# A two-block transformer kernel on one Trainium2 core: the second block's mixer as a table of steps, one convolution tap on ScalarE, one routing moved ahead

## What is computed

```python
def causal_depthwise_conv(x, w, bias):      # 4 taps, 1280 channels
    y = lax.conv_general_dilated(x, w[:, None, :].astype(x.dtype), window_strides=(1,),
                                 padding=[(CONV_WIDTH - 1, 0)],
                                 dimension_numbers=('NWC', 'WIO', 'NWC'),
                                 feature_group_count=c)
    return y + bias.astype(x.dtype)
...
    xbc = jax.nn.silu(causal_depthwise_conv(xbc, conv_w, conv_b))
...
    y = ssd_scan(xh, dt, a, bm, cm) + xh.astype(jnp.float32) * d[..., None]
    y = y.reshape(b, s, SEQ_WIDTH) * jax.nn.silu(z.astype(jnp.float32))
    return rms_norm(y, out_norm).astype(z.dtype)
...
def peer_ffn(h, w_q, sub_keys, u, v):
    q = (h @ w_q).reshape(b, s, PEER_HEADS, 2, PEER_QDIM // 2)
    scores = jnp.einsum('bshic,ikc->bshik', q, sub_keys).astype(jnp.float32)
    top_s, top_i = lax.top_k(scores, PEER_TOPK)
    cand_s = top_s[..., 0, :, None] + top_s[..., 1, None, :]
    ...
    best_s, pos = lax.top_k(cand_s, PEER_TOPK)
    expert = jnp.take_along_axis(cand_i, pos, axis=-1)
    gate = jax.nn.softmax(best_s, axis=-1).astype(h.dtype)
    ...
        act = jax.nn.gelu(jnp.einsum('td,thkd->thk', xt, u[et]), approximate=False)
        return jnp.einsum('thk,thkd->td', act * gt, v[et])
```

## Time and profile before

| | |
|---|---|
| median of 3 runs | 3017.92 us (3014.9 to 3019.11) |
| the profiled execution | 3016.67 us, its span 3014.1 us |
| busy share of the span | PE 82%, DVE 47%, ACT 30%, POOL 23% |
| DMA | 1105.16 MB, 367 GB/s over the span |
| ACT table loads | 119, 152.7 us |

### The profile page before, as it was taken

One profiled execution on the slowest core, in us unless ns is written; L12 is line 12 of the kernel. 1 busy time (PEld: TensorE's weight loads), 2 busy tenths in 40 slices (PEclk: granted clock), 3 DMA queues, 4 the chain that ended last, 5 costly groups with the idle time before them and its releaser, 6 DMA issues.

```text
span 3014.1 us, 33539 instructions
## 1 busy us (share of the span) xinstructions
PE 2473.4 (82%) x11846; PEld 1329.6 (44%) x11846; DVE 1425.9 (47%) x3374; ACT 889.7 (30%) x2348; POOL 699.4 (23%) x626
## 2 busy tenths in 40 slices
PE   9999765657999965666798998898987989877777
PEld 8776311113978421212574445454543545422222
DVE  3363100002355201000348876678657786677674
ACT  0231100000122100000235554457334583344333
POOL 4020000001211000000003553324334243444442
PEclk9999978878999988878899999999999999999999
DMA  6337999999434899999839999999999999999997
GB/s 277 126 140 306 427 428 428 428 429 404 179 130 160 367 428 427 428 427 428 359 116 415 419 413 421 422 422 416 417 422 422 417 397 415 421 422 421 420 417 308
DMA packets 123654, 1105.16 MB, mean 367 GB/s; under 512 B 13760, under 2 KB 19296, under 8 KB 23776
## 3 DMA queue, kind: packets, MB, share of 16 engines
q1 hardware_dynamic: 48032, 562.98, 44.9%
q0 software_dynamic: 73728, 536.90, 43.1%
q10 hardware_dynamic: 1728, 3.14, 0.3%
HBM read 1098.78 MB, written 4.19 MB: 366 GB/s over the span
## 4 chain that ended last, share of the span: by engine, by line
DMA 44%; PE 40%; DVE 9%; ACT 3%; issue 3%; POOL 0%; DVEq 0%; SPq 0%; ACTq 0%; POOLq 0%
DMA wbuf<-in_puv,ar 19%; PE ps L759 16%; PE ps L1583 9%; DMA wbuf<-in_w_expert_up 8%; DMA wbuf<-in_w_expert_down 8%; DMA wbuf<-in_w_expert_gate 5%; PE ps L950 4%; PE ps L1130 3%; DVE wbuf L2445 2%; PE ps L915 2%; PE ps L763 2%; ACT ar L2508 2%; ACT L2508 1%; DMA Y<-in_mem 1%; DMA wbuf<-in_w_mem_kv 1%
## 5 line engine op out<-in xcount | busy, mean ns | idle before, releaser
L1583 PE MATMUL ps<-wbuf,ar 128*128 128x512 f32 x1960 | 928.2, 612 | 188.1 <-ACT ar L2508 187.4
L2445 DVE CUSTOM_DVE_ANT_0 wbuf<-wbuf,Y 128x1024 f32<-128x1024 f32 x490 | 602.0, 1229 | 316.9 <-DMA wbuf<-in_puv,ar 308.3
L3152 POOL DMA_INDIRECT wbuf<-in_puv,ar x490 | 541.3, 1105 | 814.6 <-PE ps L1583 710.2
L1130 PE MATMUL ps<-wbuf,ar 128*32 128x512 f32 x2944 | 456.7, 756 | 293.3 <-DMA wbuf<-in_w_expert_up 112.9
L1583 PEld LDWEIGHTS ps<-wbuf,ar 128*128 128x128 f32 x1960 | 355.7, 193 | 692.0 <-issue 690.8
L2508 ACT ACTIVATE ar<-ar 128x1 f32<-128x1 f32 (+1 forms) x1051 | 269.5, 256 | 615.7 <-DVE ar L2445 592.2
L759 PE MATMUL ps<-HT,wbuf 128*128 128x128 f32 (+1 forms) x2640 | 406.3, 311 | 4.3 <-DMA wbuf<-in_w_mem_kv 3.1
L759 PEld LDWEIGHTS ps<-HT,wbuf 128*128 128x128 f32 x2640 | 368.8, 191 | 52.0 <-issue 19.9
L1130 PEld LDWEIGHTS ps<-wbuf,ar 128*32 128x32 f32 x2944 | 92.5, 124 | 642.9 <-issue 204.3
L2505 ACT COPY ar<-ps 128x512 f32<-128x512 f32 (+4 forms) x164 | 75.0, 457 | 710.5 <-PE ps L1130 307.1
L3111 POOL TENSOR_TENSOR sm<-sm,co 128x1 f32<-128x1 f32 x18 | 10.5, 582 | 1116.0 <-DVE sm L1618 1115.8
(11 more groups left out here) (206 smaller groups left out, 2064.4 us busy)
## 6 DMA issues: line engine op xcount, KB each, us to landing
wbuf<-in_w_expert_down SPq DMA_DIRECT2D x64, 2048.0 KB, 31.6
wbuf<-in_w_expert_up SPq DMA_DIRECT2D x62, 2048.0 KB, 31.5
wbuf<-in_w_expert_gate SPq DMA_DIRECT2D x58, 2048.0 KB, 30.6
wbuf<-in_w_in SPq DMA_DIRECT2D x20, 2048.0 KB, 9.0
wbuf<-in_peer_w_q SPq DMA_DIRECT2D x14, 2048.0 KB, 11.7
wbuf<-in_w_o SPq DMA_DIRECT2D x6, 2048.0 KB, 11.6
wbuf<-in_b_w_in SPq DMA_DIRECT2D x6, 2048.0 KB, 11.4
wbuf<-in_w_branch_b SPq DMA_DIRECT2D x4, 2048.0 KB, 7.9
```

The costliest lines, as they stand in the source:

```text
L1130: m = T.e.matmul(ps(jobs[n])[32 * k:32 * k + 32, :], lhs(c, k), v[:, 512 * n:512 * n + 512], start=(c == 0), stop=(c == 7), tile_position= ...
L1583: m = T.e.matmul(acc[n][:, :], DG[:, j % 4, :], rows_of(name)[:, 1024 + 512 * n:1536 + 512 * n], start=(j == 0), stop=(j == 127))
L2445: V.did(V.e.tensor_tensor_reduce(u, u, Y[:, i, :], 1.0, 0.0, ALU.mult, ALU.add, DT[:, i, j:j + 1]), f"dot{l}{i}.{j}")
L3152: G.land(G.e.indirect_dma_start(out=rows_of(name), out_offset=None, in_=I["puv"], in_offset=bass.IndirectOffsetOnAxis(ap=IX[:, i, j:j + 1] ...
```

## The change

`mix_b` becomes on each engine a table over n, the slot, of 35 slots: which step stands in which slot is written out. On PE the two tiles `x0` and `x4` are split into pairs of chunks over slots 5 to 8; `x8` goes to 9, `z4` to 10 and 11 in two parts, `z5` to 12; the memory's steps to 9 to 18 one by one; `xs` and `cb` to 16, `e` to 17 to 22, `ym` to 21 to 26, the output transposes to 31, `r0` and `r1` to 32 and 34 (from 29 and 31). On DVE the convolution stands in slots 8 to 12, two chunks each; `bEE` gets a third buffer. The tap with the newest input, and the bias, go from DVE to ACT: ten `Identity` of 128x128 from PSUM with scale and bias. And in stage (1,0), route 2 follows right behind route 1: it begins in slot 13 instead of 16.

```diff
+        def in_turn(*parts):
+            for steps in parts:
+                yield from steps
...
-        bEE = cbuf[:, 0, 0:1024].rearrange("p (k h n) -> p k h n", k=2, h=2)
+        bEE = [v.rearrange("p (h n) -> p h n", h=2)
+               for v in (cbuf[:, 0, 0:512], cbuf[:, 0, 512:1024], cbuf[:, 1, 1024:1536])]
...
+            def chunks_of(job, i, v, c0, ks, last, *names):
+                b = take(job) if ks[0] == 0 else ps(job)
+                for k in ks:
+                    m = mm(b[:, 128 * k:128 * k + 128],
+                           [(v[:, c, c0 + 128 * k:c0 + 128 * k + 128], HT[:, c, 128 * i:128 * i + 128]) for c in range(8)])
+                if last:
+                    T.did(m, job, *names)
...
+                    if n in (5, 7):
+                        chunks_of(f"{p}x{2 * n - 10}", i, tile(f"{p}w{n // 2 - 1}"), 0, (0, 1), False)
+                    if n in (6, 8):
+                        chunks_of(f"{p}x{2 * n - 12}", i, wtile(f"{p}w{n // 2 - 2}"), 0, (2, 3), True, f"{p}w{n // 2 - 2}.used")
...
+                    if n in (9, 10):
+                        unit_scores(f"b{i}m", memory[n - 9], n - 9)
+                    if n == 10:
+                        v = tile(p + "w4")
+                        b = take(p + "z4")
+                        mm(b[:, 0:256], [(Hi[c], v[:, c, 0:256]) for c in range(8)])
+                    if n == 11:
+                        T.did(mm(b[:, 256:512], [(Hi[c], v[:, c, 256:512]) for c in range(8)]), p + "z4", p + "w4.used")
+                    if n == 12:
...
+                    if n in (32, 34):
...
+                    if (l, i, q) == (1, 0, 0):
+                        nxt = in_turn(route(1, 0, 1), route(1, 0, 2))
+                    elif (l, i, q) != (1, 0, 1):
...
-                    w = [pf[:, k0 + 10 * k + c:k0 + 10 * k + c + 1] for k in range(4)]
-                    ts(bXC[:, c, :], bXR[:, c, 0:128], w[0], gain("convb", c), ALU.mult, ALU.add)
-                    for k in range(1, 4):
-                        stt(bXC[:, c, :], bXR[:, c, k:k + 128], w[k], bXC[:, c, :], ALU.mult, ALU.add,
-                            *([p + "conv"] if (c, k) == (9, 3) else []))
+                    for k in range(3):
+                        stt(bXC[:, c, :], bXR[:, c, k:k + 128], pf[:, k0 + 10 * k + c:k0 + 10 * k + c + 1], bXC[:, c, :],
...
+                    if 8 <= n < 13:
+                        convolve(i, (2 * n - 16, 2 * n - 15))
+                    if n in (10, 11):
+                        unit_max(f"b{i}m", memory[n - 10], n - 10)
...
+                    if (l, i, q) != (1, 0, 0):
+                        drain(nxt)
...
-                    copy(bXR[:, c:c + n, 3:131], ps(f"{p}x{c}")[:, 0:128 * n].rearrange("p (k t) -> p k t", k=n), f"{p}x{c}.out")
...
+                    x = ps(f"{p}x{c}")
+                    copy(bXR[:, c:c + m, 3:131], x[:, 0:128 * m].rearrange("p (k t) -> p k t", k=m))
+                    for k in range(m):
+                        w = pf[:, k0 + 30 + c + k:k0 + 31 + c + k]
+                        act(bXC[:, c + k, :], x[:, 128 * k:128 * k + 128], ACT.Identity, *([f"{p}x{c}.out"] if k + 1 == m else []),
+                            scale=w, bias=gain("convb", c + k))
...
+                    if 18 <= n < 24:
+                        hp = n - 18
+                        A.wait_ge(*at[f"{p}tm{hp}"])
+                        if hp > 2:
+                            A.wait_ge(*at[f"{p}ym{hp - 3}"])
+                        if hp == 2:
...
```

More of the change, by code:

```diff
@@ L1522, in mix_b @@
[L1522 to L1538 removed]
+                memory = with_bufs(mem_units(f"b{i}m", 1, bQM, 1), tb_b, pb_b[i])
@@ new lines, in mix_b, with residual_half @@
+                    if n == 28:
+                        mean_row(f"b{i}o", 768)
+                    if n == 29:
+                        rstd_row(f"b{i}o")
+                    if n == 30:
+                        turn_tile(f"b{i}o", i, "outn", 6)
+                    if n == 32:
+                        residual_half(i, 0)
+                    yield
+                residual_half(i, 1)
+            def residual_half(i, half):
+                p = f"b{i}."
+                V.wait_ge(*at[f"{p}r{half}"])
+                x = half_of(X, i, half)
+                tt(x, x, ps(f"{p}r{half}")[:, :], ALU.add, f"{p}r{half}.out")
@@ L2437, in stage @@
                 for q in range(4):
-                    nxt = route(l, i, q + 1) if q < 3 else iter(()) if after is None else route(l, after, 0)
+                    if (l, i, q) == (1, 0, 0):
+                        nxt = in_turn(route(1, 0, 1), route(1, 0, 2))
+                    elif (l, i, q) != (1, 0, 1):
+                        nxt = route(l, i, q + 1) if q < 3 else iter(()) if after is None else route(l, after, 0)
                     routed[0] = q == 3 and after is None
@@ L2960, in mix_b @@
-                next(memory_steps)
-                gate(4, 0, 512)
-                yield
-                drain(memory_steps)
-                yield
-                gate(5, 512, 256)
-                yield
-                yield
-                A.wait_ge(*at[p + "conv"])
-                act(bXC, bXC, ACT.Silu, p + "xc")
-                yield
-                yield
-                for c, m in ((0, 4), (4, 2)):
-                    A.wait_ge(*at[f"{p}xs{c}"])
-                    copy(bXS[:, 128 * c:128 * (c + m)], ps(f"{p}xs{c}")[:, 0:128 * m], f"{p}xs{c}.out")
@@ L2975, in mix_b @@
-                yield
-                for hp in range(1, 9):
-                    if hp < 7:
-                        hq = hp - 1
-                        k = hq % 2
-                        A.wait_ge(*at[f"{p}tm{hq}"])
-                        if hq > 1:
-                            A.wait_ge(*at[f"{p}ym{hq - 2}"])
-                        for n in range(2):
-                            h = 2 * hq + n
-                            if i == 1:
-                                act(bEE[:, k, n, 0:128], ps(f"{p}e{hq}")[:, 128 * n:128 * n + 128], ACT.Exp,
-                                    *([f"{p}e{hq}.out"] if n else []), bias=b_eb[:, h:h + 1])
-                        for n in range(2):
-                            h = 2 * hq + n
-                            act(bEE[:, k, n, 128:256], bTM[:, k, n, :], ACT.Exp, *([f"{p}ex{hq}"] if n else []),
-                                bias=b_nac[:, h:h + 1])
-                    yield
```

420 lines of the change are left out of this document (202 added, 218 removed).

## The result

The changed kernel takes **3044.8 us** (median of 5 runs, 3037.1 to 3046.2), the kernel before 3017.3 us beside it. The ratio is **1.0083, 95% interval 1.0071 to 1.0094**: slower by some 25 us by the ratio (27.5 between the medians), where 3014.3 was forecast and 3022.0 was the end of the range. The profiled execution took 3037.06 us, the fastest of the five; its span is 3035.3.

The account below looks back on a forecast made before the run. From about 1575 us the kernel was taken as a DMA stream of gathers and weight tiles, missing 8.3 us. Terms -2.2 - 0.9 - 0.5 = -3.6 us against 3016.67, plus 1.25 to the median, gave 3014.3; range 3009.0 to 3022.0.

Parts of the forecast that it names:

- Third `bEE` buffer, new waits: Decay slots: PE's `e` and DVE's mask add now share a slot; cost 0, at most the 12 slots' excess.
- -2.2 us: Stage (1,0), window 2475 to 2500: the dip heals as output products move later; 2.2 us gained, bounds 0 and -2.2.
- -0.9 us: Stage (0,1), window 2100 to 2125: products move, routing does not; half of 1.9 us gained, bounds 0 and -1.9.
- 3.73 us wait goes: Stage (1,0), gather 64: POOL's wait for its indices vanishes because the third group's routing stands three slots earlier.
- I take 0: Slots 7, 9 and 10: ten activations at 0.367 us, 3.7 us of ACT per half, cost no time.
- Projections in halves: Slots 5 to 8 at 7.3 us each on PE, DVE's slot 7 wait gone: -0.5 us, far bound -1.1.
- Starved while projecting: Rival, slots 4 to 9: later release of w3 to w5 starves the stream, 5.5 us per half, 3025.8; chance 0.12.
- The shortage only moves: Rival: lateness from the decay slots is lost all the same, there or at the product slots, 3017.9; chance 0.2.

Follow-up runs that it names:

- both edits: The changed kernel with DVE's last four steps one slot later and its emptying of the bank of `cs` in slot 9 instead of 11: 3020.30 us, ratio 1.0007.

## Why the prediction was wrong

**The step that failed** is "Third `bEE` buffer, new waits", the only place where I asked which steps of two engines had come closer together. I examined the pair I had noticed, `e` on PE and the mask on DVE in one slot, and gave the waits "Cost 0". That pair costs nothing that shows: DVE's longest wait for PE in the decay windows of half 1 is 0.47 us in the changed kernel, and with both edits the window at 2450 moves 363 where it moved 367. But the same table moves four other pairs the same way, and one the other way: the turned tile, both residual adds and `prep_tile`'s tile (DVE from one slot behind PE or level with it to level or one slot ahead), and `cs` (DVE from PE's own slot to three behind, past the slot in which PE wants its bank). None of these was costed. By the runs the output steps cost 20 us, and `cs` about 3 on top of that (not clear of noise), or 9 to 10 where the first fault stands; with both put right 1.0083 becomes 1.0007.

The numbers for it were at hand. I had worked out that a product slot holds PE for 10.8 us. DVE had its two adds one slot behind PE's products and still waited 4.07 and 6.28 us for them, in the trace of the kernel before; a slot less could be expected to make that longer: 10.64 us was seen at the first (the second, behind it, had 6.21). And "behind DVE's wait stand the next dots" was written, for `bEE` alone.

**"-2.2 us"** (the later dip heals in (1,0)). With the faults taken out, missing time in half 1 falls from 7.0 to 4.8 us, and by the run with both edits half of that is the projections' stretch and half the dip at 2475 (385 to 408, 1.4 us). So this term came out at 1.4 us in one trace, and not at all in the time: missing time over both halves goes from 9.1 to 8.8 where 3.6 less was forecast, and the ratio is 1.0007. That the decay slots stay at 6.22 us on ACT was right.

**"-0.9 us"** (half 0). Wrong in sign, as far as single traces tell: 2.1 missing before, 4.0 with both edits.

**The routing's "3.73 us wait goes".** It went, and came back at 4.21 with the routing put back; that run is no slower (0.9999 against 1.0007). So that wait was no measurable part of what the stretch loses; a share of some 3 us or less would not be seen.

**The last tap, "I take 0".** Right; 0.48 us per activation instead of 0.37 (the upper bound was twice that), no table load of their own, and no difference in time. The Trainium skill, "ScalarE: Activation LUTs", Rules for kernel authors, puts VectorE at up to about three times ScalarE's speed in bf16; no run here is in bf16, and the fp32 rows don't show such a gap: 0.48 us on ACT from PSUM against 0.382 on DVE from SBUF, a factor of 1.3.

**"Projections in halves", "-0.5 us".** DVE's 7 us wait in slot 7 is gone, and with both edits the windows from 2350 to 2425 move 419, 424 and 421 where they moved 413, 417 and 416. That is about 1 us in these two traces, the far bound of the term.

**The rivals.** "Starved while projecting" named the stretch of slots 5 to 12 and a rate under 400, and such a dip came. But its mechanism is not what made it: with the same releases of w3 to w5, and `cs` emptied two slots sooner, the window is full. A rule of decision that names only the place can be met by another cause. "The shortage only moves", 3017.9, is what the run with both edits resembles most (ratio 1.0007): dips of the decay slots are there as before once the stall ahead of them is removed, and holding tiles back moves them forward. Of the cases that I gave a chance, none had DVE waiting for PE's products.

**Still open**: how much of the 20 us belongs to the turned tile in slot 30 and how much to the four stands being close together; and why gather 64 of (0,1) waits 6.34 us in every version of the changed kernel, 1.47 before.

## What to carry to other kernels

When a program's order becomes a table, list every pair of producer and consumer across engines with its slots before and after, PSUM banks that are reused included, and cost each pair whose distance has shrunk: the wait is what the producer's slot holds it for, and everything behind the consumer on its in-order engine waits too. A stall of a few us on the engine that starts the chain (here DVE, then ACT, then PE) may cost nothing (one of 6.3 us in the kernel before), but when it is lengthened and others are added it costs most of what was added (20 us for 28). So compare the waits of the two kernels, and don't read those of one alone. In a stream bound by DMA, removing a dip can bring back another one behind it, since a stall also moves the weight tiles' loads; sum the missing time over the whole stage before adding up gains.
